# A decoder trunk on one core: which tick each segment of the next tile starts in, the tile's squares in tick 0, and the phase's sum ahead of the segment

## The chip, the core and the metric

The kernel runs on 1 core of one Trainium2 chip. The metric is the device time of one execution in microseconds (us), smaller is better. Engine names as in the profile: PE is TensorE's matmuls and PEld its weight loads, DVE is VectorE, ACT is ScalarE, POOL is GpSimd, SP is SyncE, which only issues DMAs here.

## What is computed

Two layers over 256 tokens of width 1024, everything in float32. Each layer is a mixing sub-layer (three kinds of heads over one projection) and a retrieval sub-layer (PEER): for each token 128 rows of a table of 16384 experts are fetched, weighed and added.

```python
for l in range(DEPTH):                                   # 2
    mod = silu(c) @ ada_w[l] + ada_b[l]
    h = rmsnorm(x, norm_mix_g[l]) * (1 + sc_m) + sh_m
    cols = h @ w_in[l]
    mix = concat([diff_attention(...), rwkv7_time_mix(...), forgetting_attention(...)]) @ w_out[l]
    x = x + g_m * mix
    h = rmsnorm(x, norm_ffn_g[l]) * (1 + sc_f) + sh_f
    x = x + g_f * peer_ffn(h, ...)
return rmsnorm(x, final_norm_g)

def peer_ffn(h, wq, subkeys, u_tab, v_tab):              # per token t
    eidx, gate = top 16 of the pair sums of two top 16s, for each of 8 heads
    act  = einsum('thkd,td->thk', u_tab[eidx], h)
    coef = gate * gelu(act)
    return einsum('thk,thkd->td', coef, v_tab[eidx])
```

## The kernel before

The 256 tokens are two tiles of 128, so two layers make four pairs of layer and tile, which the code calls phases (`PHASES` = 4, numbered 0 to 3). A phase fetches `SEL` = 128 expert rows for each token of its tile. One fetch brings 128 rows of 8 KB (u and v of one expert for each token, 1 MB) with an indirect DMA that GpSimd issues (L379) into a ring of `RING` = 9 slots. VectorE multiplies the u half with the hidden state and sums it (`row`, L1435), ScalarE applies the gelu (`activate`, L1042), VectorE makes the coefficient (`coefficients`, L1448), ScalarE spreads it over a diagonal (`diagonals`, L1050), and TensorE adds the v half, weighed by that diagonal, to a PSUM accumulator (`weigh`, L772). Only then is the slot free and GpSimd fetches the next row into it.

Two fetched rows make a tick, so a phase has `TICKS` = 64 of them. While phase p fetches and weighs, the same engines compute the mixing sub-layer and the retrieval's scores of the next phase's tile, cut into 79 segments (`SEGMENTS`, 0 to 78). The program of each engine is written out in Python: in tick m each engine does its part of the rows, then, through `beside.upto(PACE[m])`, its part of all segments up to number `PACE[m]`, then the rest of the tick. On VectorE the order in a tick is two rows, one part of the current tile's retrieval (ticks 0 to 23 alone, L1119 to L1157), the segments, the coefficients. On ScalarE it is the gelu, the segments, the diagonals. On TensorE it is the segments, then the weighing. Engines wait on one another by semaphores, in program order, so a wait in a segment holds everything behind it on its engine.

`pace()` makes the table from `COST`, a number for each segment. Before, segment n starts in tick `1 + 61 * done // 1783`, where `done` is the sum of the costs ahead of it. Phase 3 has no next tile; it only finishes tile 0. Phase 0's own mixing (of tile 0) runs ahead of all phases, about the first 290 us, and doesn't use this table.

The segments that the text speaks of:
- 0: ScalarE's sum of squares and square root (L809, L811), VectorE's copies. 1: VectorE's reciprocal (L1103), ScalarE's scaling (L816), TensorE's transposes (L394). 2: ScalarE and VectorE evict them (L821, L1171).
- 2 to 12, 15 to 20, 24 to 27: TensorE's projections, one group of eight matmuls each (L412); 13, 14 and 21 to 23 are the wide ones (L415). 26 is the first that needs the last group of weights, which SP loads once the projection of group `dv` (segment 23) is done (L322).
- 9: VectorE makes the squared keys (L1323) and TensorE sums them (L441). 10: VectorE takes the sums from PSUM (L1326).
- 16: VectorE's inputs for the forget gate and lambda; 17: ScalarE's exponentials and logarithm (L933 to L937).
- 28 to 30: TensorE's pair products (L482), which VectorE takes (L1192) in 29 to 31. 30 to 42: the attention and the levels of the block inverse, one unit a segment.
- 43 to 57: the state, the outputs, the output projection and the second norm. 57 to 74: the queries and scores. 75 to 77: the gate rows (L748, L795, L801).

At a phase's end, `add_sum` (L1456, L1457) reads the finished accumulator and adds it to x; it stands in tick 0 of the following phase, and TensorE's first weighing of that phase waits for it, since it reuses the accumulator.

## Time and profile before

| | us |
|---|---|
| median of 3 runs | 1900.18 |
| lowest and highest | 1897.82, 1906.14 |
| the profiled execution | 1903.03 |
| its span, first to last instruction | 1901.2 |
| PE busy | 1616.6 (85%) |
| DVE busy | 1394.7 (73%) |
| ACT busy | 673.4 (35%) |
| POOL busy | 515.2 (27%) |
| moved by DMA | 706.08 MB, mean 371 GB/s |

The profiled execution lies 2.85 us above the median. In it the first row of phase 0 is taken at 292 us; the coefficients of tick 0 of phases 0, 1, 2 and 3 end at 296.9, 725.5, 1146.7 and 1571.9 us. Busy shares are means over the whole span, and the stretches differ: the rows further down separate them.

### The profile page before, as it was taken

What the parts mean: (1) busy time and instruction counts of PE and PEld (TensorE: products, weight loads), DVE (VectorE), ACT (ScalarE), POOL (GpSimd) and SP (SyncE); (2) the same over time, 40 slices, a digit from 0 to 9 for tenths busy, and PEclk for the clock granted to TensorE, in tenths of its full rate; (3) what the DMA queues carried; (4) which work ended last, traced back from release to release, by engine and by line L of the source; (5) the groups of instructions that cost most, each with busy time, mean ns of one, the idle gap of its engine ahead of it and who ended that gap; (6) DMA issues with size and microseconds to landing.
All of it is one profiled execution on the core that took longest, in us unless ns stands there. A gap on an engine that the chain in (4) does not pass through costs nothing.

```text
span 1901.2 us, 20926 instructions
## 1 busy us (share of the span) xinstructions
PE 1616.6 (85%) x6868; PEld 1006.0 (53%) x6868; DVE 1394.7 (73%) x3315; ACT 673.4 (35%) x1640; POOL 515.2 (27%) x564
## 2 busy tenths in 40 slices
PE   1767678898999998898999998898999997887776
PEld 1656665554665655564665655554665652332222
DVE  5866598997856758998765748988765759985554
ACT  1313114334732334335632235325632233331112
POOL 2000013222233232222233232222232233343331
PEclk9889788998999999998999999999999998999999
DMA  9982688997799999998999999998899999999996
GB/s 393 422 346 101 242 353 348 367 421 286 283 399 421 422 420 395 363 422 313 321 403 421 421 421 399 370 402 293 287 403 421 421 415 401 416 407 421 421 421 256
DMA packets 96989, 706.08 MB, mean 371 GB/s; under 512 B 10992, under 2 KB 11504, under 8 KB 13296
## 3 DMA queue, kind: packets, MB, share of 16 engines
q0 software_dynamic: 80640, 587.24, 77.1%
q1 hardware_dynamic: 16240, 117.50, 15.1%
q8 instruction: 55, 0.90, 0.2%
q14 instruction: 54, 0.44, 0.1%
HBM read 703.64 MB, written 1.05 MB: 371 GB/s over the span
## 4 chain that ended last, share of the span: by engine, by line
PE 49%; DVE 28%; DMA 16%; ACT 3%; issue 3%; POOL 0%; DVEq 0%; ACTq 0%; POOLq 0%
PE psum L772 26%; DMA ringmem<-in_peer_uv_dram,eidx 11%; DVE ringmem L1435 9%; PE psum L648 5%; PE psum L412 4%; DMA W<-in_w_groups_dram 3%; PE psum L635 2%; DMA ringmem<-in_ada_pairs_dram 2%; PE psum L520 1%; PE psum L508 1%; DVE ringmem L1079 1%; PE psum L518 1%; PE psum L415 1%; DVE coef L1448 1%; ACT diag L1050 1%
## 5 line engine op out<-in xcount | busy, mean ns | idle before, releaser
L772 PE MATMUL psum<-ringmem,diag 128*128 128x512 f32 x2048 | 978.4, 624 | 132.3 <-ACT diag L1050 132.0
L379 POOL DMA_INDIRECT ringmem<-in_peer_uv_dram,eidx x512 | 489.5, 956 | 1131.5 <-PE psum L772 1079.7
L1435 DVE SCALAR_TENSOR_TENSOR ringmem<-ringmem,psum 128x1024 f32<-128x1024 f32 x512 | 612.5, 1220 | 195.3 <-DMA ringmem<-in_peer_uv_dram,eidx 180.1
L772 PEld LDWEIGHTS psum<-ringmem,diag 128*128 128x128 f32 x2048 | 389.1, 199 | 608.1 <-issue 409.1
L1050 ACT ACTIVATE diag<-K,coef 128x128 f32<-128x128 f32 x512 | 176.4, 393 | 225.8 <-DVE coef L1448 225.6
L412 PE MATMUL psum<-hT,W 128*128 128x128 f32 x1344 | 172.3, 287 | 40.9 <-DMA W<-in_w_groups_dram 19.1
L412 PEld LDWEIGHTS psum<-hT,W 128*128 128x128 f32 x1344 | 169.2, 203 | 64.9 <-issue 38.0
L1042 ACT ACTIVATE coef<-dots 128x2 f32<-128x2 f32 x256 | 51.8, 202 | 408.6 <-DVE ringmem L1435 407.7
L1079 DVE SCALAR_TENSOR_TENSOR ringmem<-ringmem,diag 128x1024 f32<-128x1024 f32 x96 | 115.3, 1223 | 20.9 <-DMA ringmem<-in_ada_pairs_dram 18.8
L648 PEld LDWEIGHTS psum<-hT,W 128*128 128x128 f32 x1024 | 123.2, 197 | 12.8 <-issue 7.2
L648 PE MATMUL psum<-hT,W 128*128 128x128 f32 x1024 | 126.0, 281 | 3.1 <-ACT hT L821 3.0
L1042 ACT ACT_TABLE_LOAD x80 | 102.6, 1283 | 1.4
L1448 DVE SCALAR_TENSOR_TENSOR coef<-coef,ginv,gexp 128x2 f32<-128x2 f32 x256 | 57.1, 223 | 47.5 <-ACT coef L1042 41.1
L370 POOL DMA_DIRECT2D ringmem<-in_ada_pairs_dram x48 | 25.5, 536 | 222.2 <-DVE ringmem L1079 221.4
L635 PE MATMUL psum<-W,hT 128*128 128x256 f32 x256 | 60.3, 393 | 0.8 <-issue 0.8
L635 PEld LDWEIGHTS psum<-W,hT 128*128 128x128 f32 x256 | 50.6, 198 | 13.7 <-issue 6.9
L1208 DVE COPY_PREDICATED W<-K,psum 128x384 f32<-128x384 int32 x32 | 18.7, 585 | 47.3 <-PE psum L553 47.3
L866 ACT ACTIVATE attn<-attn,ast 128x128 f32<-128x128 f32 (+1 forms) x64 | 28.7, 449 | 54.4 <-DVE ast L1223 53.7
L394 PE MATMUL psum<-K,hm 128*128 128x128 f32 x96 | 15.4, 313 | 38.2 <-ACT hm L816 27.9
L415 PE MATMUL psum<-W,hT 128*128 128x260 f32 (+1 forms) x128 | 41.0, 467 | 7.2 <-DMA W<-in_w_groups_dram 7.2
L1012 ACT ACTIVATE ar<-psum 128x256 f32<-128x256 f32 x32 | 12.2, 382 | 94.0 <-PE psum L648 94.0
L1192 DVE TENSOR_TENSOR W<-psum,K 128x512 f32<-128x512 f32 x24 | 16.6, 691 | 38.0 <-PE psum L482 37.5
(243 smaller groups left out, 1629.7 us busy)
## 6 DMA issues: line engine op xcount, KB each, us to landing
ringmem<-in_ada_pairs_dram POOLq DMA_DIRECT2D x48, 1024.0 KB, 19.0
W<-in_w_pieces_dram SPq DMA_DIRECT2D x48, 1024.0 KB, 9.2
W<-in_w_groups_dram SPq DMA_DIRECT2D x24, 1536.0 KB, 11.3
W<-in_w_groups_dram SPq DMA_DIRECT2D x12, 1024.0 KB, 9.6
ringmem<-in_peer_uv_dram,eidx POOLq DMA_INDIRECT x512, 11.7
W<-in_w_groups_dram SPq DMA_DIRECT2D x4, 1040.0 KB, 9.2
attn<-in_subkeys_t_dram SPq DMA_DIRECT2D x4, 1024.0 KB, 9.5
K<-in_consts_dram SPq DMA_DIRECT2D x1, 1546.0 KB, 18.1
```

What stands on the lines that cost most here:

```text
L379: nc.gpsimd.indirect_dma_start(slot(k), None, rows, bass.IndirectOffsetOnAxis(ap=eidx[:, ph % 2, m:m + 1], axis=0)).then_inc(row_landed[q ...
L412: mm = nc.tensor.matmul(group_bank(g)[:, j * P:(j + 1) * P], wt[:, k, j * P:(j + 1) * P], hT[:, k, :], start=(k == 0), stop=(k == KD - 1))
L415: mm = nc.tensor.matmul(group_bank(g)[:, 0:w], hT[:, k, :], wt[:, k, 0:w], start=(k == 0), stop=(k == KD - 1))
L635: mm = nc.tensor.matmul(bank[6 + j // 2][:, (j % 2) * 256:(j % 2 + 1) * 256], hT[:, k, :], wpiece[j % 3][:, k, :], start=(k == 0), stop=(k ...
L648: mm = nc.tensor.matmul(bank[6 + h % 2][:, a * P:(a + 1) * P], wpiece[j % 3][:, k, a * P:(a + 1) * P], hT[:, k, :], start=(k == 0), stop=( ...
L772: mm = nc.tensor.matmul(acc[:, q], diag[:, k % DIAGS, :], slot(k)[:, D:][:, q], start=(k % SEL == 0), stop=(k % SEL == SEL - 1), skip_grou ...
L866: ins = nc.scalar.activation(sc[:, n % 2, a, 0:nk], sc[:, n % 2, a, 0:nk], exp, bias=ast[:, n % 4, a:a + 1], scale=DIFF_SCALE if kind == " ...
L1042: nc.scalar.activation(coef[:, q], dots[:, q], gelu).then_inc(s["gelu_out"], 1)
L1050: ins = nc.scalar.activation(diag[:, k % DIAGS, :], ident, ACT.Copy, scale=coef[:, j:j + 1])
L1079: ins = v.scalar_tensor_tensor(out=u, in0=u, scalar=1.0, in1=crow, op0=ALU.mult, op1=ALU.mult, accum_out=MC[:, l, SECTIONS[r // KD], r % K ...
L1435: ins = v.scalar_tensor_tensor(out=u, in0=u, scalar=1.0, in1=hrep, op0=ALU.mult, op1=ALU.mult, accum_out=dots[:, j:j + 1])
L1448: step(v.scalar_tensor_tensor(out=coef[:, q], in0=coef[:, q], scalar=ginv[:, ph % 2, h:h + 1], in1=gexp[:, ph % 2, m * BATCH:(m + 1) * BAT ...
```

## The change

`pace()` now uses 62 instead of 61, has no 1 added, and lets each of the fourteen segments named in `CHAINED` start at least one tick after the segment ahead of it. On VectorE `add_sum` moves ahead of the segments of tick 0.

```diff
--- before.py
+++ after.py
@@ -96,11 +96,15 @@
 assert len(COST) == SEGMENTS
 
 
+
+CHAINED = {1, 2, 43, 44, 45, 46, 47, 48, 49, 50, 51, 55, 56, 57}
+
+
 def pace():
 
-    total, done, out = sum(COST), 0, [-1] * TICKS
+    total, done, tick, out = sum(COST), 0, 0, [0] * TICKS
     for n, w in enumerate(COST):
-        tick = 1 + (TICKS - 3) * done // total
+        tick = max((TICKS - 2) * done // total, tick + (n in CHAINED))
         for m in range(tick, TICKS):
             out[m] = n
         done += w
@@ -1487,9 +1491,9 @@
                             row(k)
                         if m < 4 * (PH - 2):
                             retrieve(ph, 2 + m // 4, m % 4)
-                        beside.upto(PACE[m])
                         if m == 0 and ph:
                             add_sum(ph - 1)
+                        beside.upto(PACE[m])
                         coefficients(n)
                 add_sum(PHASES - 1)
                 finish_tile(1)
```

What the table becomes (segments by tick):

| tick | 0 | 1 | 2 | 3 | 4 | 5 | 6 | 7 | 8 | 9 | 10 | 11 |
|---|---|---|---|---|---|---|---|---|---|---|---|---|
| before | | 0, 1, 2 | 3 | 4, 5 | 6 | 7 | 8, 9 | 10 | 11, 12 | 13 | 14 | 15, 16 |
| now | 0 | 1 | 2, 3, 4 | 5, 6 | 7 | 8 | 9, 10 | 11 | 12, 13 | 14 | 15 | 16, 17 |

| tick | 12 | 13 | 14 | 15 | 16 | 17 | 18 | 19 | 20 | 21 | 22 | 23 | 24 | 25 |
|---|---|---|---|---|---|---|---|---|---|---|---|---|---|---|
| before | 17 | 18 | 19 | 20, 21 | 22 | 23, 24 | 25, 26 | 27, 28 | 29 | 30 | 31 | 32 | 33 | 34 |
| now | 18 | 19 | 20, 21 | 22 | 23, 24 | 25, 26 | 27 | 28, 29 | 30 | 31 | 32 | 33 | 34 | |

Ticks 26 to 30 hold segments 35 to 39 in both. Before, tick 31 is empty and 40 to 45 stand in ticks 32 to 37, 46 and 47 together in tick 38. Now 40 to 46 stand in ticks 31 to 37 and 47 alone in 38. From there on the tables differ by at most one tick, and by the gate rows at the end: 75 in tick 60 and 76, 77 in tick 61 before, 75 and 76 in tick 60 and 77 in tick 61 now. Of the pairs that `CHAINED` takes apart, only 0, 1, 2 and 46, 47 shared a tick before.

**ScalarE where segment 0 of a next tile stands** (here the start of phase 1; L1042 is the gelu and L1050 the diagonals of a tick, L809 and L811 segment 0, L816 segment 1, L821 segment 2). Before:

```order
L1042 ACTIVATE coef<-dots 128x2
L1050 ACTIVATE diag<-K,coef 128x128 x2
L1042 ACTIVATE coef<-dots 128x2
L809 ACTIVATE hm,stat<-xs 128x1024
L811 ACT_TABLE_LOAD
L811 ACTIVATE stat<-stat 128x1
L816 ACTIVATE hm<-xs,stat 128x1024
L821 ACTIVATE hT<-psum,MC 128x128 x4
L1050 ACTIVATE diag<-K,coef 128x128 x2
L1042 ACT_TABLE_LOAD
```

Now (line numbers four higher: L1046, L1054, L813, L815, L820, L825):

```order
L1046 ACTIVATE coef<-dots 128x2
L813 ACTIVATE hm,stat<-xs 128x1024
L815 ACT_TABLE_LOAD
L815 ACTIVATE stat<-stat 128x1
L1054 ACTIVATE diag<-K,coef 128x128 x2
L1046 ACT_TABLE_LOAD
L1046 ACTIVATE coef<-dots 128x2
L820 ACTIVATE hm<-xs,stat 128x1024
L1054 ACTIVATE diag<-K,coef 128x128 x2
L1046 ACTIVATE coef<-dots 128x2
L825 ACTIVATE hT<-psum,MC 128x128 x4
```

The squares and the square root stand between the gelu and the diagonals of tick 0; the scaling and the eviction follow in ticks 1 and 2.

**TensorE over the same ticks and up to the sums of the keys** (L772 is the weighing, x4 is one tick; L394 the transposes, L412 the projections, L430 and L436 the low-rank inputs and the gate, L441 the key sums). Before:

```order
L412 MATMUL psum<-hT,W 128x128 x8
L772 MATMUL psum<-ringmem,diag 128x512 x4
L412 MATMUL psum<-hT,W 128x128 x16
L772 MATMUL psum<-ringmem,diag 128x512 x4
L412 MATMUL psum<-hT,W 128x128 x8
L430 MATMUL psum<-attn,lora 128x128 x3
L430 MATMUL psum<-mixed,lora 128x128 x3
L772 MATMUL psum<-ringmem,diag 128x512 x4
L412 MATMUL psum<-hT,W 128x128 x8
L436 MATMUL psum<-lora,attn 128x384
L772 MATMUL psum<-ringmem,diag 128x512 x4
L412 MATMUL psum<-hT,W 128x128 x16
L441 MATMUL psum<-T,K 128x384
```

Now (L776, L416, L434, L440, L445):

```order
L416 MATMUL psum<-hT,W 128x128 x16
L434 MATMUL psum<-attn,lora 128x128 x3
L434 MATMUL psum<-mixed,lora 128x128 x3
L776 MATMUL psum<-ringmem,diag 128x512 x4
L416 MATMUL psum<-hT,W 128x128 x8
L440 MATMUL psum<-lora,attn 128x384
L776 MATMUL psum<-ringmem,diag 128x512 x4
L416 MATMUL psum<-hT,W 128x128 x8
L776 MATMUL psum<-ringmem,diag 128x512 x4
L416 MATMUL psum<-hT,W 128x128 x8
L445 MATMUL psum<-T,K 128x384
L416 MATMUL psum<-hT,W 128x128 x8
```

The projections of one more segment stand ahead of each of the early weighings, a projection of the following segment stands behind the key sums in the same tick, and VectorE's reader of the sums is in this tick too, as the next rows show.

**VectorE around the sums of the keys** (L1323 writes the squares, L1326 reads the sums, L1448 ends a tick, L1435 begins the next). Before:

```order
L1182 SCALAR_TENSOR_TENSOR mixed<-mixed,pcols,colsT 128x128 x3
L1322 TENSOR_TENSOR T<-mixed,pcols 128x384
L1323 TENSOR_TENSOR T<-T 128x384
L1448 SCALAR_TENSOR_TENSOR coef<-coef,ginv,gexp 128x2
L1435 SCALAR_TENSOR_TENSOR ringmem,dots<-ringmem,psum 128x1024 x2
L1144 TENSOR_SCALAR fhi<-fpos 128x16
```

Now (L1327, L1330, L1452, L1439):

```order
L1186 SCALAR_TENSOR_TENSOR mixed<-mixed,pcols,colsT 128x128 x3
L1326 TENSOR_TENSOR T<-mixed,pcols 128x384
L1327 TENSOR_TENSOR T<-T 128x384
L1330 TENSOR_SCALAR T<-psum 128x384
L1333 SCALAR_TENSOR_TENSOR attn<-AL,pcols 128x384
L1334 SCALAR_TENSOR_TENSOR attn<-attn,mixed 128x384
L1452 SCALAR_TENSOR_TENSOR coef<-coef,ginv,gexp 128x2
L1439 SCALAR_TENSOR_TENSOR ringmem,dots<-ringmem,psum 128x1024 x2
```

The reader of the sums, which stood behind two rows and a retrieval part of the next tick, now stands directly behind the writer of the squares.

## Rows read from the trace of the kernel before

**Rows 1.** Stretches: the front (ticks 0 to 35) and back (36 to 63) of phases.
```profile
core 0: us, PE busy (x) PEld busy (x) DVE busy (x) ACT busy (x) POOL busy (x), PEclk, DMA share, GB/s
296.90:533.00 236.10, 217.89 (x948) 135.97 (x949) 198.22 (x501) 116.26 (x256) 63.72 (x66) 0.95 0.89 345
...
725.50:963.70 238.20, 220.51 (x968) 138.51 (x969) 202.10 (x520) 117.04 (x267) 65.76 (x69) 0.95 0.92 360
963.70:1146.70 183.00, 168.70 (x743) 106.36 (x741) 115.14 (x262) 55.20 (x147) 55.44 (x59) 0.99 1.01 420
1146.70:1389.70 243.00, 225.01 (x988) 141.01 (x989) 202.66 (x511) 118.51 (x263) 65.42 (x68) 0.95 0.90 350
```

**Rows 2.** The chain that ended last, phase 3, two fetches 16 ticks apart (start, length).
```profile
1758.26 15.10 DMA ringmem<-in_peer_uv_dram,eidx
...
1838.05 15.41 DMA ringmem<-in_peer_uv_dram,eidx
```

**Rows 3.** Timeline of ticks 0 and 1 of phase 1, engine by engine.
```profile
723.79 1.23 DVE L1457 TENSOR_TENSOR xs<-xs,hm 128x1024 f32<-128x1024 f32 x1
...
730.86 0.16 DVE L1103 RECIPROCAL stat<-stat 128x1 f32<-128x1 f32 x1 [0.59 <-ACT stat L811]
733.89 1.36 DVE L1171 TENSOR_SCALAR hT<-psum,MC 128x128 f32<-128x128 f32 x4 [2.87 <-PE psum L394]
...
728.02 1.04 ACT L809 ACTIVATE hm<-xs 128x1024 f32<-128x1024 f32 x1
...
729.17 1.28 ACT L811 ACT_TABLE_LOAD   x1
730.46 0.29 ACT L811 ACTIVATE stat<-stat 128x1 f32<-128x1 f32 x1
...
726.25 6.66 PE L772 MATMUL psum<-ringmem,diag 128*128 128x512 f32 x8 [5.08 <-ACT diag L1050]
...
735.36 2.02 PE L412 MATMUL psum<-hT,W 128*128 128x128 f32 x16 [1.58 <-ACT hT L821]
```

**Rows 4.** Timeline of PE, ticks 29 to 31: one weighing, then two back to back.
```profile
931.94 3.70 PE L772 MATMUL psum<-ringmem,diag 128*128 128x512 f32 x8
...
938.68 7.13 PE L772 MATMUL psum<-ringmem,diag 128*128 128x512 f32 x16
```

**Rows 5.** Timeline of PE and DVE around the sums of the keys, phase 1.
```profile
769.30 0.81 PE L441 MATMUL psum<-T,K 128*128 128x384 f32 x2
...
767.76 0.56 DVE L1323 TENSOR_TENSOR T<-T 128x384 f32<-128x384 f32 x1
...
774.38 0.56 DVE L1326 TENSOR_SCALAR T<-psum 128x384 f32<-128x384 f32 x1
```

**Rows 6.** Timeline of ACT, segment 17 in tick 12 of phase 1.
```profile
814.98 1.28 ACT L937 ACT_TABLE_LOAD   x1
```

**Rows 7.** Timeline of SP, PE and DVE around the last weight load, phase 1.
```profile
845.61 0.33 SPq L322 DMA_DIRECT2D W<-in_w_groups_dram  x1
...
854.74 3.48 PE L412 MATMUL psum<-hT,W 128*128 128x128 f32 x16 [2.16 <-DMA W<-in_w_groups_dram]
858.01 3.86 PE L772 MATMUL psum<-ringmem,diag 128*128 128x512 f32 x8
...
864.82 1.42 DVE L1192 TENSOR_TENSOR W<-psum,K 128x512 f32<-128x512 f32 x2 [6.55 <-PE psum L482]
```

**Rows 8.** Timeline of DVE, the ends of ticks 4 and 5 of phase 1.
```profile
753.10 0.22 DVE L1448 SCALAR_TENSOR_TENSOR coef<-coef,ginv,gexp 128x2 f32<-128x2 f32 x1
...
757.48 0.22 DVE L1448 SCALAR_TENSOR_TENSOR coef<-coef,ginv,gexp 128x2 f32<-128x2 f32 x1
```

**Rows 9.** The page's group of VectorE's row products: busy, mean ns.
```profile
L1435 DVE SCALAR_TENSOR_TENSOR ringmem<-ringmem,psum 128x1024 f32<-128x1024 f32 x512 | 612.5, 1220 | 195.3 <-DMA ringmem<-in_peer_uv_dram,eidx 180.1
```

**Rows 10.** Timeline of PE, the end of phase 3: the last gate row, the last three weighings.
```profile
1876.55 1.16 PE L748 MATMUL psum<-hm,ones 128*128 128x128 f32 x8 [0.85 <-ACT hm L795]
1878.97 12.26 PE L772 MATMUL psum<-ringmem,diag 128*128 128x512 f32 x24 [1.26 <-ACT diag L1050]
```

## The prediction

> **What bounds the kernel now.** I read the stretches by clock time first, since shares over the whole span mix unlike parts. A phase has a front, ticks 0 to 35, in which the transfers run at 345 to 360 GB/s, and a back, ticks 36 to 63, at 420 [rows 1]. In the front the ring is often full of landed rows that wait for VectorE and TensorE, so the DMA engines run dry; in the back VectorE waits for rows. The chain of waits shows what a tick costs when only transfers count: in phase 3 two fetches that stand 16 ticks apart begin at 1758.26 and 1838.05 us, so a tick is 4.99 us [rows 2]. Bytes are unchanged, so the time changes by what is added to or taken from the dry time of the fronts, and by the tail. One phase is worked out, phase 1; phases 0 and 2 have the same table and the same kinds of wait.
>
> **What a shift of the table is worth by itself.** The attention and the block inverse, which end the front, now stand one tick earlier: the last unit, segment 42, is in tick 33 instead of 34. So one tick without new work leaves the front and is done in the back. In the front it costs TensorE, which is busy there for 220.5 of 238.2 us [rows 1] and in the attention almost without a break, one weighing: two back to back take 7.13 where one takes 3.70, so 3.43 us [rows 4]. In the back it costs 4.99 us [rows 2]. This alone is 4.99 - 3.43 = +1.6 us a phase. It is the unobvious part: work done earlier in a tick count isn't done earlier in time if the tick it leaves was cheap.
>
> **The waits, as TensorE sees them at equal segments.**
>
> 1. Squares in tick 0. ScalarE now waits for the phase's sum (VectorE ends it at 723.79 + 1.23 = 725.02), then does squares, table load and root, which took 728.02 to 730.75, so 2.73 us, and only then the diagonals that release the first weighing. Before, the weighing began at 726.25, 1.23 behind the sum, with coefficients and diagonals in between. The coefficients (some 0.5 of it) can run beside the squares, the diagonals can't: 2.73 + 0.73 - 1.23, so 2.2, and I take 2.3 for a handover more; bounds 1.5 and 2.7. TensorE already waits 5.08 there [rows 3]. VectorE isn't held, its rows have landed.
> 2. What that removes: in tick 1 TensorE waited 1.58 for the evicted transposes and VectorE 0.59 + 2.87 = 3.46 for root and transposes [rows 3]. Both go. TensorE's net of items 1 and 2 is +0.7.
> 3. The key sums. VectorE wrote their input at 767.76 + 0.56 = 768.3 and read the sums at 774.38, behind the rows and a retrieval part of the next tick; TensorE made them from 769.30 to 770.1 [rows 5]. Now VectorE reads directly behind the write. It arrives 3.46 sooner, at 764.9 or, with smaller new waits for ScalarE's gelu and low-rank work in ticks 2 to 5, which I bound by 0 and 1.5, up to 766.4. TensorE has the same six weighings and projections ahead, so it is done at 770.1 + 0.7 = 770.8. VectorE thus waits about 5 us, more than it gained in tick 1; the gain of tick 1 is given back here. While it waits, the diagonals of tick 6 stand behind it. For TensorE the waits of ticks 6 to 10 stay about the same; I take -0.6, bounds -2 and +2.
> 4. Segments 16 and 17 share tick 11. ScalarE's exponential needs VectorE's result and TensorE's second transposes of the same tick, and then two table loads of 1.28 stand ahead of the diagonals [rows 6]. Before, segment 17 had a tick to itself, where the gate's exponential had loaded the first table. The order has three more table loads, one a phase. I take 2.3 us (1.28, the load, and 1.0 for the order within the tick), bounds 0 and 3.8 (the load, and one more load's length for each side of the handover).
> 5. The last weight load. SP issues it at 845.61 when group `dv` is done, TensorE starts on it at 854.74 after 2.16 of waiting [rows 7]. Segments 23 and 26 stay one tick apart, so this wait stays: 0.
> 6. Segments 30 to 33 now fall in ticks 20 to 23 and meet VectorE's last retrieval parts; before, 33 was in tick 24, free of them. VectorE picks up with the pair products (before at 864.82 [rows 7]) and then bounds these ticks. One more part must be done before segment 33: a tick with a part and no segment is 757.48 - 753.10 = 4.38 [rows 8], less two row products of 1.22 [rows 9] and the coefficients' 0.22, so 1.7. TensorE is also handed the pair products and the masks in one tick each; I take 2.2 in all, bounds 0 and 4.
>
> Sum a phase: 1.6 + 0.7 - 0.6 + 2.3 + 0 + 2.2 = +6.2 us, for three phases +18.6. Splitting 46 from 47 lies in the back, where transfers bound: 0. `add_sum` ahead of segment 0 puts VectorE's copies (under 0.5 us) behind the sum instead of into tick 1: 0; without the move ScalarE's squares would wait a little longer.
>
> **The tail.** Phase 3 has no segments but the gate rows. The second one ran at 1876.55, in tick 61, and the last three weighings ran back to back from 1878.97 to 1891.23, 12.26 us [rows 10]. With both gate rows in tick 60, the weighing of 61 can start sooner; the last rows set the end then: -1.7, bounds -2 and 0.
>
> **Sum.** 1903.03 + 18.6 - 1.7 = 1919.9 for the profiled execution, which is 2.85 above the median; so **1917 us**.
>
> **A rule weighed.** The table loads took 1.28 us, and the root began 0.01 after the load's end (729.17 + 1.28 = 730.45, then 730.46) [rows 3]. The Trainium skill (ScalarE: Activation LUTs, What ACT_TABLE_LOAD costs) gives 1283 ns and a drain of about 1380 ns, 2.66 us for a switch. The row shows no drain. By the page the three added loads would cost 4.1 us more, an estimate, and the sum would be about 1921.
>
> **Rivals.**
>
> A. *No net change* (1894 to 1908, likeliest 1901). New waits fall into VectorE's or TensorE's existing ones: the waits of items 4 and 6 are hidden by TensorE's backlog, and the shift's +1.6 is all that stays: 3 x 1.6 - 1.7 = +3. For it: TensorE trails VectorE by some microseconds through ticks 11 to 20, and backlog hides releases. Against it: in tick 20 the trail ends, VectorE waits 6.55 for TensorE [rows 7].
>
> B. *Faster, through tick 1* (about 1888). The wait of 3.46 on VectorE [rows 3] is really gone and isn't given back, because TensorE reaches the key sums sooner than item 3 has it. Then VectorE is 3.5 ahead, SP issues the last load that much earlier, and the wait of 2.16 [rows 7] goes too: 1.6 - 3.5 - 2.2 = -4.1 a phase, -12.3 and the tail. It decides if VectorE's wait for the key sums stays under 1.5 us. For it: TensorE's 1.58 goes. The Trainium skill (Perfetto Trace Analysis, Optimization Strategies) speaks for it: where TensorE idles for other engines, shorten what blocks it. Here the trace agrees only in that tick; the hold of item 1 lengthens another of TensorE's idle times.
>
> C. *The change hardly does what it says* (within 3 us of 1900). Of fourteen names only two groups shared a tick before. The shift of the others is real, though, as the order shows, so this is weak.
>
> **How the numbers follow.** My forecast 0.50 (1909 to 1930: bounds of items 3, 4 and 6 together), A 0.26, B 0.20, C 0.04. A measurement of this kernel can tell 0.5%, 9.5 us, from no change. Faster by over 0.5%: B and a little of A, 0.20. Slower by over 0.5%: the forecast with a little left off at its low end and a little of A added, 0.51. Within: 0.29. The range leaves out half of B below 1888 and the forecast's end above 1930: 1888 to 1930; the forecast's own is 1909 to 1930.
>
> **What would show it.** Right: VectorE has waits of 4 to 6 us for L445 in tick 6 of each phase; no wait at L1175 in tick 1 of more than 0.5; TensorE's first weighing of phases 1 and 2 begins about 2.3 later against the end of the sum; the coefficients of tick 35 come 5 to 8 us later after those of tick 0; the backs keep 420 GB/s. Wrong: fronts shorter than 236 to 243 us [rows 1] at equal ticks, a wait for L445 under 1.5, or dry transfers in the back. A back with waits on TensorE while rows lie landed would make the whole split by front and back wrong.

## The result and the profile after

| | us |
|---|---|
| before, median of 4 runs | 1899.0 (1897.1 to 1906.1) |
| the changed kernel, median of 4 runs | 1921.3 (1920.9 to 1922.8) |
| ratio, 95% interval | 1.0102, 1.0082 to 1.0122 |
| profiled execution and its span, before | 1903.0, 1901.2 |
| profiled execution and its span, after | 1920.9, 1919.1 |

The changed kernel is slower by 1.0%, some 19 us. The forecast was 1917. Where the 17.9 us between the two spans lie can be read from the ends of the coefficients (L1448 before, L1452 after) of tick 0 and tick 35 of each phase:

| | before | after | longer by |
|---|---|---|---|
| start to tick 0 of phase 0 | 296.9 | 300.0 | 3.1 |
| phase 0, to tick 0 of phase 1 | 428.6 | 432.3 | 3.7 |
| of it ticks 0 to 35 | 244.2 | 246.9 | 2.7 |
| phase 1, to tick 0 of phase 2 | 421.2 | 427.3 | 6.0 |
| of it ticks 0 to 35 | 236.0 | 241.6 | 5.6 |
| phase 2, to tick 0 of phase 3 | 425.2 | 428.9 | 3.7 |
| of it ticks 0 to 35 | 244.2 | 247.6 | 3.4 |
| phase 3, to the last coefficients | 313.1 | 315.0 | 1.9 |
| from there to the end | 16.2 | 15.7 | -0.5 |

So 13.4 us were lost in the three phases that have segments, 11.7 of them in the fronts. The 3.1 ahead of phase 0 and the 1.9 in phase 3 lie where both kernels run the same instructions, apart from the squares in tick 0 and the gate rows; the last section comes back to them. The fronts of this table end with the coefficients of tick 35; the windows of [rows 1] end elsewhere, that of phase 0 at 533.0 where tick 35 ends at 541.1, so its 236.10 is not comparable with the 244.2 here.

Stretches of the changed kernel's phase 1, front and back, as in [rows 1]; the columns are PE, PEld, DVE, ACT and POOL busy, then the granted clock, the DMA share and GB/s:

```profile
732.30:974.10 241.80, 219.76 (x968) 137.76 (x969) 199.81 (x517) 118.23 (x267) 64.61 (x68) 0.94 0.90 350
974.10:1159.50 185.40, 168.72 (x742) 105.99 (x740) 116.97 (x264) 54.83 (x149) 56.52 (x60) 1.00 1.01 421
```

The back still runs at 421 GB/s, and the front is longer with the same work: TensorE is busy for 219.8 us of 241.8, against 220.5 of 238.2 [rows 1]. The loss is waiting.

Timeline of the start of phase 1 after the change (start, length, engine, line; in brackets the idle time before it and what ended it):

```profile
729.93 1.23 DVE L1461 TENSOR_TENSOR xs<-xs,hm 128x1024 f32<-128x1024 f32 x1
...
742.58 1.37 DVE L1175 TENSOR_SCALAR hT<-psum,MC 128x128 f32<-128x128 f32 x4
...
731.18 1.06 ACT L813 ACTIVATE hm<-xs 128x1024 f32<-128x1024 f32 x1 [4.04 <-DVE xs L1461]
...
732.35 1.28 ACT L815 ACT_TABLE_LOAD   x1
733.65 0.29 ACT L815 ACTIVATE stat<-stat 128x1 f32<-128x1 f32 x1
733.85 0.68 ACT L1054 ACTIVATE diag<-K,coef 128x128 f32<-128x128 f32 x2
...
734.58 5.92 PE L776 MATMUL psum<-ringmem,diag 128*128 128x512 f32 x8 [6.83 <-ACT diag L1054]
```

The phase's sum ends at 731.16 and the first weighing begins at 734.58, 3.42 behind it; before it was 726.25 - 725.02 = 1.23 [rows 3]. So item 1 costs 2.2, as forecast. And L1175, which waited 2.87 in tick 1 before [rows 3], now takes the transposes in tick 2 and waits for nothing.

Timeline of ticks 6 and 7 of phase 1 after the change, VectorE and then TensorE:

```profile
770.92 0.56 DVE L1327 TENSOR_TENSOR T<-T 128x384 f32<-128x384 f32 x1
775.62 0.56 DVE L1330 TENSOR_SCALAR T<-psum 128x384 f32<-128x384 f32 x1 [4.15 <-PE psum L445]
...
785.58 2.55 DVE L1338 RECIPROCAL T<-T 128x384 f32<-128x384 f32 x1
...
789.35 0.22 DVE L1452 SCALAR_TENSOR_TENSOR coef<-coef,ginv,gexp 128x2 f32<-128x2 f32 x1
...
774.70 0.81 PE L445 MATMUL psum<-T,K 128*128 128x384 f32 x2
775.35 1.95 PE L416 MATMUL psum<-hT,W 128*128 128x128 f32 x16
778.40 3.70 PE L776 MATMUL psum<-ringmem,diag 128*128 128x512 f32 x8 [1.10 <-ACT diag L1054]
781.94 1.95 PE L416 MATMUL psum<-hT,W 128*128 128x128 f32 x16
790.35 5.35 PE L776 MATMUL psum<-ringmem,diag 128*128 128x512 f32 x8 [6.46 <-ACT diag L1054]
```

VectorE stands 4.15 us for the keys' sums, and one tick later TensorE stands 6.46 for the diagonals, which wait for VectorE's coefficients at 789.57. That wait is an old one: TensorE of the kernel before, ticks 7 to 9 of phase 1:

```profile
777.16 3.70 PE L772 MATMUL psum<-ringmem,diag 128*128 128x512 f32 x8 [1.83 <-ACT diag L1050]
780.70 3.73 PE L412 MATMUL psum<-hT,W 128*128 128x128 f32 x32
789.84 5.59 PE L772 MATMUL psum<-ringmem,diag 128*128 128x512 f32 x8 [5.41 <-ACT diag L1050]
795.26 1.92 PE L415 MATMUL psum<-W,hT 128*128 128x260 f32 x8
```

In tick 8 TensorE waits 5.41 for VectorE. The prediction never looked at this row, and it is the one that decided two of its items.

TensorE of the changed kernel in ticks 21 to 23 of phase 1, where the attention meets VectorE's last retrieval parts:

```profile
885.01 0.71 PE L537 MATMUL psum<-dk,dq 64*128 64x128 f32 x4 [1.86 <-DVE ast L1227]
886.51 6.75 PE L776 MATMUL psum<-ringmem,diag 128*128 128x512 f32 x8 [0.79 <-ACT diag L1054]
...
901.21 0.94 PE L512 MATMUL psum<-W 128*128 128x128 f32 x6 [2.08 <-DVE W L1204]
...
903.16 1.22 PE L537 MATMUL psum<-dk,dq 64*128 64x128 f32 x4 [0.62 <-DVE ast L1227]
904.65 6.22 PE L776 MATMUL psum<-ringmem,diag 128*128 128x512 f32 x8 [0.28 <-ACT diag L1054]
```

VectorE bounds these ticks, and two weighings that took 3.70 elsewhere [rows 4] took 6.75 and 6.22 behind the waits. The kernel before has two slow ones there as well, of 5.36 and 5.40.

### The profile page after: what moved, and what is told of

It reads as the page before. It is cut to its first block, busy times and chain, and to the rows that moved or that the text cites. A ratio compares the mean times of both kernels' runs of the same rounds, so it can differ in the third digit from the quotient of the medians.

```text
span 1919.1 us, 20926 instructions
## 1 busy us (share of the span) xinstructions
PE 1619.7 (84%) x6868; PEld 1009.7 (53%) x6868; DVE 1394.0 (73%) x3315; ACT 678.6 (35%) x1643; POOL 517.6 (27%) x564
## 4 chain that ended last, share of the span: by engine, by line
PE 53%; DVE 23%; DMA 17%; ACT 3%; issue 3%; POOL 0%; DVEq 0%; ACTq 0%; POOLq 0%
PE psum L776 29%; DMA ringmem<-in_peer_uv_dram,eidx 12%; DVE ringmem L1439 7%; PE psum L416 5%; PE psum L652 4%; DMA W<-in_w_groups_dram 3%; PE psum L639 2%; DMA ringmem<-in_ada_pairs_dram 2%; PE psum L419 2%; PE psum L524 1%; DVE ringmem L1083 1%; PE psum L512 1%; PE psum L522 1%; PE psum L752 1%; DVE W L1196 1%
## 5 line engine op out<-in xcount | busy, mean ns | idle before, releaser
L776 PE MATMUL psum<-ringmem,diag 128*128 128x512 f32 x2048 | 976.3, 623 | 140.3 <-ACT diag L1054 140.0
L1439 DVE SCALAR_TENSOR_TENSOR ringmem<-ringmem,psum 128x1024 f32<-128x1024 f32 x512 | 613.2, 1220 | 236.4 <-DMA ringmem<-in_peer_uv_dram,eidx 219.9
L776 PEld LDWEIGHTS psum<-ringmem,diag 128*128 128x128 f32 x2048 | 388.6, 198 | 614.0 <-issue 407.2
L1054 ACT ACTIVATE diag<-K,coef 128x128 f32<-128x128 f32 x512 | 176.4, 393 | 201.9 <-DVE coef L1452 197.9
L1046 ACT ACTIVATE coef<-dots 128x2 f32<-128x2 f32 x256 | 51.9, 203 | 469.0 <-DVE ringmem L1439 462.3
L416 PE MATMUL psum<-hT,W 128*128 128x128 f32 x1344 | 168.0, 282 | 34.5 <-DVE hT L1175 17.2
L416 PEld LDWEIGHTS psum<-hT,W 128*128 128x128 f32 x1344 | 165.2, 198 | 59.6 <-issue 37.7
L1452 DVE SCALAR_TENSOR_TENSOR coef<-coef,ginv,gexp 128x2 f32<-128x2 f32 x256 | 57.0, 222 | 49.9 <-ACT coef L1046 43.8
L1439 DVE DVE_READ_ACCUMULATOR ringmem<-ringmem,psum 128x1 f32 x512 | 42.3, 83 | 0.0
L512 PE MATMUL psum<-W 128*128 128x128 f32 x240 | 36.3, 291 | 7.1 <-DVE W L1204 7.1
```

The costliest lines, as they stand in the source:

```text
L416: mm = nc.tensor.matmul(group_bank(g)[:, j * P:(j + 1) * P], wt[:, k, j * P:(j + 1) * P], hT[:, k, :], start=(k == 0), stop=(k == KD - 1))
L512: mm = nc.tensor.matmul(bank[5][:, j * P:(j + 1) * P], AT[b][:, 0:P], X[:, b, :], start=True, stop=True)
L776: mm = nc.tensor.matmul(acc[:, q], diag[:, k % DIAGS, :], slot(k)[:, D:][:, q], start=(k % SEL == 0), stop=(k % SEL == SEL - 1), skip_grou ...
L1046: nc.scalar.activation(coef[:, q], dots[:, q], gelu).then_inc(s["gelu_out"], 1)
L1054: ins = nc.scalar.activation(diag[:, k % DIAGS, :], ident, ACT.Copy, scale=coef[:, j:j + 1])
L1439: ins = v.scalar_tensor_tensor(out=u, in0=u, scalar=1.0, in1=hrep, op0=ALU.mult, op1=ALU.mult, accum_out=dots[:, j:j + 1])
```

## The experiments

`pace()` can be written as a plain list of each segment's tick. In the experiments it is (`BEGINS`, with `return [sum(s <= m for s in BEGINS) - 1 for m in range(TICKS)]`), and each diff shows the lines of that list that differ: a line that begins with 0 holds segments 0 to 25, one that begins with 17 or 18 segments 26 to 51. All runs stood beside runs of the kernel before on the same chip; the ratio is to those.

| run | base | edit | median us | ratio, 95% interval |
|---|---|---|---|---|
| `e_chain` | before | 0, 1, 2 in ticks 0, 1, 2; sum ahead | 1890.8 | 0.9951, 0.9932 to 0.9969 |
| `e_keys` | changed | 10 in tick 7 | 1910.4 | 1.0049, 1.0032 to 1.0066 |
| `e_gate` | changed | 17 in tick 12 | 1923.3 | 1.0120, 1.0102 to 1.0138 |
| `e_attn` | changed | 29 to 34 and 40 to 46 a tick later | 1899.2 | 0.9991, 0.9979 to 1.0003 |
| `b_pairs` | before | 29 to 34 a tick earlier | 1915.4 | 1.0083, 1.0062 to 1.0104 |
| `b_outputs` | before | 40 to 46 a tick earlier | 1907.1 | 1.0034, 1.0021 to 1.0048 |
| `a_sum` | changed | sum behind the segments | 1923.1 | 1.0119, 1.0100 to 1.0139 |
| `e_both` | changed | `e_keys` and `e_attn` | 1886.3 | 0.9933, 0.9912 to 0.9954 |
| `e_root` | `e_both` | 2 in tick 1 | 1896.7 | 0.9976, 0.9966 to 0.9986 |
| `e_early` | `e_both` | 40 to 46 a tick earlier | 1891.0 | 0.9939, 0.9921 to 0.9957 |
| `e_late` | `e_chain` | 29 to 39 a tick later | 1888.4 | 0.9937, 0.9916 to 0.9958 |
| `e_free` | `e_both` | 29 to 39 a tick later | 1876.6 | 0.9863, 0.9844 to 0.9883 |

In what follows a difference of two ratios is given in us of 1900; each is uncertain by 4 to 5.

### The split of the chain alone

```diff
-        1, 1, 1, 2, 3, 3, 4, 5, 6, 6, 7, 8, 8, 9, 10, 11, 11, 12, 13, 14, 15, 15, 16, 17, 17, 18,
+        0, 1, 2, 2, 3, 3, 4, 5, 6, 6, 7, 8, 8, 9, 10, 11, 11, 12, 13, 14, 15, 15, 16, 17, 17, 18,
...
-                        beside.upto(PACE[m])
                         if m == 0 and ph:
                             add_sum(ph - 1)
+                        beside.upto(PACE[m])
```

> The kernel before with the sum ahead of the segments and segments 0, 1 and 2 in ticks 0, 1 and 2; all the others where they were. Theory T (the loss comes from the segments that were moved a tick earlier, and the split of the chain is a small cost on TensorE in tick 0 against a wait gone in tick 1): 1897 to 1903 us, within 0.3% of the kernel before; VectorE and TensorE have no wait over 0.5 us for the squares in tick 1, and the keys' sums are read one tick after they are written with no long wait. Rival B (VectorE's 3.5 us of waiting in tick 1 was worth its length in each phase): 1888 or less. Rival H (the squares in front of the first weighing are what costs): 1907 or more.

Measured 1890.8, 9 us faster than before. My theory and its value fell, and the value of B was near, but not by B's whole path: the wait for the last weights, which B took away, is still 2.01 in phase 1 of this run. The wait of tick 8 after this edit, TensorE, phase 1:

```profile
784.62 5.73 PE L771 MATMUL psum<-ringmem,diag 128*128 128x512 f32 x8 [5.05 <-ACT diag L1049]
```

Against the end of the coefficients of tick 0 (724.29, before 725.47) this weighing begins at 60.33, before at 64.37: 4.0 earlier. The gain stood at 1.6 from tick 3 to 6, became 4.0 in tick 8 and stayed that to the end of the phase. In phase 0 it is 1.5 and then 3.6. In phase 2 the weighings of ticks 3 to 6 come 0.5 later, and from tick 8 on 3.1 earlier. So VectorE's gain in tick 1 reaches TensorE in full, at the place where TensorE waits for VectorE.

### Which of the two waits in tick 1 it was

`e_root` puts segment 2 back beside 1; it is cut from `e_both` (below), which holds the split of the chain and no wait for the keys.

```diff
-        0, 1, 2, 2, 2, 3, 3, 4, 5, 6, 7, 7, 8, 8, 9, 10, 11, 11, 12, 13, 14, 14, 15, 16, 16, 17,
+        0, 1, 1, 2, 2, 3, 3, 4, 5, 6, 7, 7, 8, 8, 9, 10, 11, 11, 12, 13, 14, 14, 15, 16, 16, 17,
```

> e_both with segments 1 and 2 together in tick 1 (0 stays in tick 0). It parts the two waits of VectorE in tick 1 of the kernel before: 0.59 for the root stays away, 2.87 for the transposes comes back. Theory V (VectorE bounds tick 8, so what it gains in tick 1 arrives there in full): 2 to 3.5 us a phase more than e_both, 1893 to 1897. Rival (TensorE's idle time for the first weighing decides, and VectorE's waits in tick 1 are covered): 1885 to 1889.

Measured 1896.7, by ratio 8 us slower than `e_both`. VectorE in tick 1 of phase 1:

```profile
730.58 1.36 DVE L1174 TENSOR_SCALAR hT<-psum,MC 128x128 f32<-128x128 f32 x4 [5.24 <-PE psum L397]
```

With the squares in tick 0 TensorE is later, so the wait for its transposes is 5.24 where it was 2.87. Against `e_both` the coefficients of ticks 6 to 20 come 5.3 to 5.6 later and the first weighing that shows the whole of it is that of tick 7; 3.5 are left at the end of the phase; the three phases are 4.9, 3.5 and 5.1 longer. VectorE's time ahead of tick 7 is worth its length there, and it is the transposes' wait that the split pays by; the root's 0.59 is away in `e_root` too.

### The sum's place

```diff
-                        if m == 0 and ph:
-                            add_sum(ph - 1)
                         beside.upto(PACE[m])
+                        if m == 0 and ph:
+                            add_sum(ph - 1)
```

> The changed kernel with the sum behind the segments again, where the kernel before had it; nothing else. By the forecast (VectorE's copies of under 0.5 us stand ahead of the sum, and ScalarE's squares, if they follow the sum, wait that much longer): +0.5 us a phase over three phases, 1921 to 1924 us. If ScalarE's squares no longer wait for the sum: up to 3 us less a phase, 1912 or more. If the copies hold nothing: 1921.

Measured 1923.1, by ratio 3 us slower than the changed kernel, which its interval does not part from none. In phase 1 the weighings of ticks 1 to 9 come 0.7 to 0.8 later. That is all that can be put down to the move: over whole phases the run is 4.6 longer in phase 0, which has no sum to move, 1.0 shorter in phase 1 and 1.9 longer in phase 2.

### The keys' sums

```diff
-        0, 1, 2, 2, 2, 3, 3, 4, 5, 6, 6, 7, 8, 8, 9, 10, 11, 11, 12, 13, 14, 14, 15, 16, 16, 17,
+        0, 1, 2, 2, 2, 3, 3, 4, 5, 6, 7, 7, 8, 8, 9, 10, 11, 11, 12, 13, 14, 14, 15, 16, 16, 17,
```

> The changed kernel with segment 10 in tick 7 instead of 6, so that VectorE reads the keys' sums one tick after it writes the squares. Theory T as forecast (item 3: the wait of 4 to 5 us on VectorE is hidden by TensorE's backlog): 1919 to 1923 us, no change. Rival K (that wait holds the diagonals of tick 6 and the rows behind it, and TensorE loses with it): 2 to 4 us less a phase, 1909 to 1915.

Measured 1910.4, by ratio 10 us faster than the changed kernel. My item 3 fell, K holds. VectorE takes the sums without a wait, and TensorE's next wait is shorter:

```profile
771.58 0.56 DVE L1329 TENSOR_SCALAR T<-psum 128x384 f32<-128x384 f32 x1
...
780.17 3.70 PE L775 MATMUL psum<-ringmem,diag 128*128 128x512 f32 x8 [3.47 <-ACT diag L1053]
```

3.47 where it was 6.46. In phase 1 the weighings of ticks 8 to 10 come 3.8 to 4.1 earlier than in the changed kernel: the 4.15 of L1330. Not all of it stays: from tick 12 on it is 2.1, and the three phases are 1.8, 1.8 and 3.6 shorter, 7.2 in all where the ratio says 10.

### The gate's two segments in one tick

```diff
-        0, 1, 2, 2, 2, 3, 3, 4, 5, 6, 6, 7, 8, 8, 9, 10, 11, 11, 12, 13, 14, 14, 15, 16, 16, 17,
+        0, 1, 2, 2, 2, 3, 3, 4, 5, 6, 6, 7, 8, 8, 9, 10, 11, 12, 12, 13, 14, 14, 15, 16, 16, 17,
```

> The changed kernel with segment 17 in tick 12 instead of 11, so that the forget gate's inputs and its exponentials have a tick of their own each. As forecast in item 4, worth 2.3 us a phase: 1914 us, between 1910 and 1921. If the tick's wait is made up later (the weighings stood 3.4 later in tick 11 but coefficients only 0.6 to 1.9 in ticks 11 and 12): 1920 to 1922.

Measured 1923.3: nothing gained, if anything 3 lost. The wait of item 4 is there in the changed kernel, as ScalarE and TensorE of tick 11 show:

```profile
817.58 1.28 ACT L937 ACT_TABLE_LOAD   x1
...
819.19 1.28 ACT L941 ACT_TABLE_LOAD   x1
...
821.33 3.70 PE L776 MATMUL psum<-ringmem,diag 128*128 128x512 f32 x8 [2.17 <-ACT diag L1054]
```

TensorE stands 2.17 in tick 11, and with the edit that weighing comes 2.4 earlier after the coefficients of tick 0. But the weighing of tick 12 comes where it came: segment 17's own work now stands there and takes what was won. Item 4's 2.3 us a phase was the price of one tick, not of the phase. The run also has six table loads fewer than the changed kernel, 174 against 180, and is no faster.

### The later segments: pairs and attention

```diff
-        17, 18, 19, 19, 20, 21, 22, 23, 24, 26, 27, 28, 29, 30, 31, 32, 33, 34, 35, 36, 37, 38, 39, 40, 41, 42,
+        17, 18, 19, 20, 21, 22, 23, 24, 25, 26, 27, 28, 29, 30, 32, 33, 34, 35, 36, 37, 38, 38, 39, 40, 41, 42,
```

> The changed kernel with segments 29 to 46 one tick later, where the kernel before had them. By items 6 and the shift of the forecast this gives back 2.2 + 1.6 us a phase, in all 11 us: 1910 us (1904 to 1916). If the loss is made ahead of tick 19 and only shows there: 1918 to 1922.

Measured 1899.2: all of the loss is gone, 21 us, twice what items 6 and the shift were held to be worth. Two kernels cut it from the other side. `b_pairs`, from the kernel before:

```diff
-        18, 19, 19, 20, 21, 22, 23, 24, 25, 26, 27, 28, 29, 30, 32, 33, 34, 35, 36, 37, 38, 38, 39, 40, 41, 42,
+        18, 19, 19, 19, 20, 21, 22, 23, 24, 26, 27, 28, 29, 30, 32, 33, 34, 35, 36, 37, 38, 38, 39, 40, 41, 42,
```

> The kernel before with segments 29 to 34 alone one tick earlier (29 now shares tick 19 with 27 and 28, and the free tick moves from 31 ahead to 25; both stay). By item 6 of the forecast 2.2 us a phase, in all +7: 1907 us. By e_attn's trace, whose loss of 5 us a phase against the changed kernel stands between ticks 19 and 26: +10 to +15, 1910 to 1915. If the pieces only cost together with segments 9 to 28 being early: under +4.

Measured 1915.4, 16 us slower than before; the forecast's 2.2 a phase is half of what it costs, or less. Its trace says why. VectorE in tick 19 and TensorE in ticks 21 and 22, phase 1:

```profile
869.92 1.42 DVE L1191 TENSOR_TENSOR W<-psum,K 128x512 f32<-128x512 f32 x2 [11.21 <-PE psum L481]
...
884.17 0.71 PE L532 MATMUL psum<-dk,dq 64*128 64x128 f32 x4 [1.87 <-DVE ast L1222]
...
891.24 0.52 PE L494 MATMUL psum<-K,W 128*128 128x128 f32 x3 [1.87 <-DVE W L1199]
```

Segment 29 takes the pair products that TensorE makes in the same tick. VectorE, a tick ahead, has to stand 11.21 for them, and in tick 20 the wait of 6.55 [rows 7] is not taken again. What is worse, the following ticks are VectorE's (two rows, a retrieval part and a unit of the attention; ticks 21 to 23 take 7.0 to 9.5 us each), and it enters them later. In phase 1 the weighings of ticks 22 and 23 come 6.6 to 6.9 later than before, and 3.7 of it stays.

The changed kernel itself doesn't show 11.21. There the projections are a tick earlier too, and its wait has to be held against that of `e_attn`, the same kernel with the pairs back where the kernel before has them. The changed kernel and then `e_attn`, VectorE, phase 1:

```profile
870.77 1.42 DVE L1196 TENSOR_TENSOR W<-psum,K 128x512 f32<-128x512 f32 x2 [6.53 <-PE psum L486]
```

```profile
866.14 1.42 DVE L1195 TENSOR_TENSOR W<-psum,K 128x512 f32<-128x512 f32 x2 [2.13 <-PE psum L485]
```

So in phase 1 the shared tick adds 4.4 to this wait here and 4.7 between `b_pairs` and the kernel before; in phases 0 and 2 it is 2.5 to 4.3. At tick 30 the loss is 5.2, 3.7 and 4.1 in phases 0 to 2 by `b_pairs` and 2.6, 5.1 and 5.6 by `e_attn`, 13 in all both times, beside the 16 of the ratio. No run moves segment 29 alone, so how much of it is this wait and how much the units that meet VectorE's last retrieval parts stays open.

`b_outputs`, the shift with no other effect:

```diff
-        18, 19, 19, 20, 21, 22, 23, 24, 25, 26, 27, 28, 29, 30, 32, 33, 34, 35, 36, 37, 38, 38, 39, 40, 41, 42,
+        18, 19, 19, 20, 21, 22, 23, 24, 25, 26, 27, 28, 29, 30, 31, 32, 33, 34, 35, 36, 37, 38, 39, 40, 41, 42,
```

> The kernel before with segments 40 to 46 alone one tick earlier, so tick 31 is no longer free of segments. By the forecast's first term (a cheap tick leaves the front, 1.6 us a phase): +5, 1905 us. If a shift inside the front that adds no wait costs nothing: 1899 to 1902.

Measured 1907.1, 6.5 us slower, near the forecast's 4.8. But its profiled execution doesn't show where: phases 0 to 2 are 0.6 and 0.6 longer and 0.6 shorter than before. So it was measured a second time on another base, `e_both`, with the same edit:

```diff
-        17, 18, 19, 20, 21, 22, 23, 24, 25, 26, 27, 28, 29, 30, 32, 33, 34, 35, 36, 37, 38, 38, 39, 40, 41, 42,
+        17, 18, 19, 20, 21, 22, 23, 24, 25, 26, 27, 28, 29, 30, 31, 32, 33, 34, 35, 36, 37, 38, 39, 40, 41, 42,
```

> e_both with segments 40 to 46 one tick earlier, the second measure of the shift alone. If b_outputs' 6.7 us are the shift's own: 1892 to 1894. If they are not, as its trace says (its phases 0 to 2 are 0.6, 0.6 and -0.6 us longer than those of the kernel before): 1885 to 1889.

Measured 1891.0, between the two; by ratio 1.1 us slower than `e_both`. From tick 31 on, where the edit begins, its phases 0, 1 and 2 are 1.8, 0.3 and 0.1 longer. A third reading is `e_attn`, which gives back 1.4, 1.3 and 3.8 behind tick 30. The shift alone is a loss of 1 to 6 us in all. That it is one is likely, and its size stays open.

### Both repairs, and what is left of the change

```diff
-        0, 1, 2, 2, 2, 3, 3, 4, 5, 6, 6, 7, 8, 8, 9, 10, 11, 11, 12, 13, 14, 14, 15, 16, 16, 17,
-        17, 18, 19, 19, 20, 21, 22, 23, 24, 26, 27, 28, 29, 30, 31, 32, 33, 34, 35, 36, 37, 38, 39, 40, 41, 42,
+        0, 1, 2, 2, 2, 3, 3, 4, 5, 6, 7, 7, 8, 8, 9, 10, 11, 11, 12, 13, 14, 14, 15, 16, 16, 17,
+        17, 18, 19, 20, 21, 22, 23, 24, 25, 26, 27, 28, 29, 30, 32, 33, 34, 35, 36, 37, 38, 38, 39, 40, 41, 42,
```

> The changed kernel with both edits that gained: segment 10 in tick 7 and segments 29 to 46 one tick later. Against the kernel before it still has the split of the chain and segments 3 to 9 and 11 to 28 up to one tick earlier. Theory T (three separate terms: chain -10, sums of the keys +11, segments 29 to 46 +22; the rest of the shift costs nothing): 1888 to 1893 us, as e_chain. Theory U (the earlier segments 11 to 28 also cost, and only overlap with the other two): 1894 or more. If the two edits give back the same wait: 1899.

Measured 1886.3, 13 us faster than before and 3 to 4 faster than `e_chain`. The terms are separate and add up. What `e_both` has beyond `e_chain` costs nothing that shows and may gain a little: most of segments 3 to 8 and 11 to 28 stand a tick earlier, so that 16 and 17 share one, and so do five segments of the back and one gate row. Its front of phase 1 beside [rows 1]:

```profile
718.70:950.00 231.30, 215.71 (x962) 135.59 (x963) 199.04 (x515) 118.07 (x266) 64.84 (x68) 0.96 0.93 369
```

### One tick more between the pairs and the attention

`e_late` puts segments 29 to 39 a tick later in `e_chain`, so that the tick without a segment is 20 and not 31:

```diff
-        18, 19, 19, 20, 21, 22, 23, 24, 25, 26, 27, 28, 29, 30, 32, 33, 34, 35, 36, 37, 38, 38, 39, 40, 41, 42,
+        18, 19, 19, 21, 22, 23, 24, 25, 26, 27, 28, 29, 30, 31, 32, 33, 34, 35, 36, 37, 38, 38, 39, 40, 41, 42,
```

> e_chain with segments 29 to 39 one tick later, so that the free tick stands at 20 instead of 31. Theory T (VectorE's last retrieval parts and its wait for the pair products make ticks 20 to 23 the dearest; each tick that the pairs move away from them gives back): 3 to 5 us a phase less than e_chain, 1877 to 1882. Rival (in e_chain the trail is already free at tick 20, so an empty tick there is worth what one at 31 is): 1889 to 1893. Rival (VectorE's wait of 6.5 us in tick 20 stays, for the pair products of segment 28 are late for TensorE's own reasons): 1886 to 1890.

Measured 1888.4, 2 to 3 us faster than `e_chain`, which is not parted from none. VectorE in tick 20 of its phase 1:

```profile
859.83 0.22 DVE L1447 SCALAR_TENSOR_TENSOR coef<-coef,ginv,gexp 128x2 f32<-128x2 f32 x1 [7.86 <-ACT coef L1041]
```

ScalarE ahead of it:

```profile
857.20 0.38 ACT L846 ACTIVATE fk<-psum 128x256 f32<-128x256 f32 x1 [9.90 <-PE psum L411]
```

The wait for the pairs only changed its name: VectorE now stands 7.86 for ScalarE's gelu, which stands behind ScalarE's eviction of TensorE's last projection. In `e_both` the projections are a tick earlier, and there the same edit is `e_free`:

```diff
-        17, 18, 19, 20, 21, 22, 23, 24, 25, 26, 27, 28, 29, 30, 32, 33, 34, 35, 36, 37, 38, 38, 39, 40, 41, 42,
+        17, 18, 19, 21, 22, 23, 24, 25, 26, 27, 28, 29, 30, 31, 32, 33, 34, 35, 36, 37, 38, 38, 39, 40, 41, 42,
```

> e_both with segments 29 to 39 one tick later, so that the tick free of segments is 20 and not 31. Theory W (TensorE's waits of 1.9, 0.8 and 0.8 us in ticks 22 and 23 of e_both come from VectorE's last retrieval parts there, and the attention's first units leave them): 1 to 2 us less a phase, 1880 to 1884. Rival (as in e_late, the waits move with the units and only change their place): 1885 to 1888.

Measured 1876.6 over 4 runs, 13 us by ratio faster than `e_both` and 26 faster than the kernel before; more than W held. Its profiled execution, of 1883.6, is the longest of the four, so the trace shows less of it: phase 0 is 1.3 longer and phases 1 and 2 are 2.8 and 1.7 shorter than those of `e_both`. VectorE's wait for the pairs, 2.0 to 2.2 a phase in `e_both`, is gone. Where the rest of the 13 lies was not seen. TensorE in ticks 22 to 24 of phase 1:

```profile
871.14 3.70 PE L775 MATMUL psum<-ringmem,diag 128*128 128x512 f32 x8
874.68 0.49 PE L498 MATMUL psum<-K,W 128*128 128x128 f32 x3
877.73 0.71 PE L536 MATMUL psum<-dk,dq 64*128 64x128 f32 x4 [2.56 <-DVE ast L1226]
879.23 5.40 PE L775 MATMUL psum<-ringmem,diag 128*128 128x512 f32 x8 [0.79 <-ACT diag L1053]
884.46 0.49 PE L498 MATMUL psum<-K,W 128*128 128x128 f32 x3
```

One such wait, and one slow weighing, are left where the kernel before and the changed kernel each had two slow weighings. This is the version that beats both.

## Why the time was right and half of the sum was not

The sign, the size (1917 against 1921) and the place, the fronts of phases 0 to 2, came as forecast. The sum behind it did not: its terms were wrong in both directions and met in the total, and that they met is luck. In us over the three phases:

| term | forecast | measured by |
|---|---|---|
| items 1 and 2, split of the chain | +2.1 | -9 (`e_chain`) |
| item 3, keys' sums | -1.8 | +10 (`e_keys`) |
| item 4, gate | +6.9 | 0, or -3 (`e_gate`) |
| item 6, pairs and attention | +6.6 | +16 (`b_pairs`) |
| shift of 40 to 46 alone | +4.8 | +1 to +6 (`e_early`, `b_outputs`) |
| rest of the shift, with item 4 and the tail in it | 0 | -3 (`e_both` less `e_chain`) |
| tail | -1.7 | none seen |

The right column, with item 4 counted once, adds up to between 15 and 20, against 19 by the ratio; each entry is uncertain by 4 to 5.

Of the signs that the prediction named, VectorE's wait for L445 is there in each phase (4.0, 4.2 and 4.7), the wait at L1175 is gone, the first weighings of phases 1 and 2 stand 2.2 later against the sum, and the backs keep 419 to 421 GB/s. One sign failed: tick 35 was to come 5 to 8 us later in each phase and came 2.7, 5.6 and 3.4 later. Phase 1, the one worked out, was the dearest. So the phases carry 13.4 of the 18.6 that they were given, and a good part of the rest of the 17.9 between the two spans lies where nearly the same instructions run.

**Items 1 and 2.** The hold itself was right: 2.2 us measured in the trace. The step that failed is "TensorE's net of items 1 and 2 is +0.7": by `e_chain` the weighings of ticks 3 to 6 come 1.5 and 1.6 earlier in phases 0 and 1, and only phase 2 has 0.5 later. It priced the chain on TensorE in ticks 0 and 1 and dropped VectorE's 3.46 as if it had slack. But TensorE waits for VectorE in ticks 7 and 8 (1.83 and 5.41), so VectorE's time ahead of tick 8 counts in full. `e_chain` and `e_root` show it, in opposite directions.

**Item 3.** The wait was forecast well (about 5, measured 4.15), and so was its cause. The step that failed is "For TensorE the waits of ticks 6 to 10 stay about the same". It compared VectorE's arrival with TensorE's in tick 6 alone. The sentence before it, that the gain of tick 1 is given back here, was right, and together items 1 to 3 came near: forecast +0.3, measured about +1. So two errors were one: a gain and a loss on VectorE, both taken for nothing.

**Item 4.** The mechanism is in the trace (two loads of 1.28, a wait of 2.17), but the tick after hides it. It should have been asked which wait ends last in the next tick.

**Item 5** held. The same wait for the last weights is in the changed kernel, one tick earlier, TensorE and the granted clock of the stretch behind it:

```profile
858.90 2.05 PE L416 MATMUL psum<-hT,W 128*128 128x128 f32 x16 [2.11 <-DMA W<-in_w_groups_dram]
...
858.90:861.00 2.10, 2.10 (x17) 2.08 (x18) 2.07 (x6) 0.39 (x3) 0.00 (x0) 1.00 1.04 433
```

2.11 of waiting, before 2.16 [rows 7].

**Item 6** had the right place and half the size or less: 2.2 a phase, measured 4.3 to 5.3. The step that failed is the count of VectorE's work in ticks 20 to 23 as the whole price. It left out that segment 29 now shares a tick with the products that it reads, which adds 4.4 to VectorE's wait in phase 1 (6.53 against 2.13 in `e_attn`) before those ticks begin.

**The shift** of 1.6 a phase is in keeping with both measurements and shown by neither.

**The tail.** Both gate rows now stand in tick 60, but TensorE reaches its last weighings no sooner. Ends of the two kernels, the sum's first instruction before and after:

```profile
1891.33 1.23 DVE L1456 TENSOR_TENSOR hm<-psum,grow 128x1024 f32<-128x1024 f32 x1 [6.32 <-PE psum L772]
```

```profile
1892.59 1.91 PE L752 MATMUL psum<-hm,ones 128*128 128x128 f32 x8 [1.85 <-ACT hm L799]
1894.29 14.85 PE L776 MATMUL psum<-ringmem,diag 128*128 128x512 f32 x32
...
1909.24 1.22 DVE L1460 TENSOR_TENSOR hm<-psum,grow 128x1024 f32<-128x1024 f32 x1 [5.77 <-PE psum L776]
```

The second gate row's matmuls run back to back with four weighings instead of three [rows 10]. From the last coefficients to the end it is 0.5 us shorter, but `b_pairs` and `e_chain`, which have the gate rows of the kernel before, are 1.7 and 1.1 shorter there. From tick 0 of phase 3 to the end the five kernels with the old rows take 328.9 to 332.0 and the nine with the new ones 329.4 to 332.1. So no gain shows, and none of 1.7 came.

**The rivals.** A asked for hidden waits, and item 4's was hidden, but not those on VectorE. B named its condition, VectorE's wait for the keys under 1.5 us. The wait was 4.15, so B did not come. But the condition doesn't decide it alone: in `e_keys`, which makes just that true, the kernel runs at 1910, since B had no term for the pairs. Only with the pairs back in their tick as well, in `e_both`, is it 1886, near B's 1888. And the wait for the last weights, for which B took 2.2 a phase away, is in all fourteen kernels, 2.0 to 3.7 in each phase, so B's number was met by another sum.

**The sums themselves.** B's terms with the tail give 1903.0 - 12.3 - 1.7 - 2.85 = 1886, not 1888, and A's +3 gives 1903, not 1901. The bounds of items 3, 4 and 6 together span 1899 to 1935, not 1909 to 1930; the result lies in both.

**The rule of the Trainium skill on table loads** (ScalarE: Activation LUTs, What ACT_TABLE_LOAD costs) would add a drain of about 1.4 us to each load. The trace after disagrees as that of before did: L815's load ends at 732.35 + 1.28 = 733.63 and the root begins at 733.65. Over all loads of either trace ScalarE's median idle time is 0.02 ahead of a load and 0.01 behind it. That the sum with the drain, about 1921, is what was measured is chance, since no drain shows in either trace. The other rule of the Trainium skill, to shorten what blocks an idle TensorE (Perfetto Trace Analysis, Optimization Strategies), agrees with `e_chain`, though the wait that the edit shortened on VectorE was paid out seven ticks later.

## What to carry to other kernels

When engines run one in-order schedule, price a change of one engine's time at the next place where the bounding engine waits for it, not in the tick where it happens: look down the trace for the first long wait with that engine's name. A table that moves many segments by one tick is many edits; run its pieces alone, since here a gain of 9 and losses of 10 and 16 lay in one change of 19. And leave a tick between a product and its reader where the reader's engine runs ahead: the keys' sums show it alone, the pairs together with the units behind them.

## What was not expected of the hardware

**The clock behind a wait is not the wait's alone.** Stretches of 2 to 7 us in which TensorE ran right behind a wait, first the last weights of the kernel before, then two of the changed kernel (the granted clock is the third number from the end, of which 1.00 is 2.4 GHz):

```profile
854.70:858.30 3.60, 3.56 (x17) 3.56 (x18) 3.38 (x12) 0.00 (x0) 0.00 (x0) 0.56 1.03 428
```

```profile
790.40:795.80 5.40, 5.40 (x11) 2.48 (x12) 5.12 (x16) 1.79 (x4) 0.94 (x1) 0.69 0.00 0
...
886.50:893.30 6.80, 6.79 (x10) 2.90 (x11) 6.35 (x19) 2.74 (x3) 0.95 (x1) 0.54 0.55 187
```

After a wait of 2.16 sixteen matmuls took 3.48 at 0.56, nearer to the lower level of 1.2 GHz than to the upper; after one of 2.11, in the changed kernel, they took 2.05 at 1.00. A weighing took 5.35 behind a wait of 6.46 and 6.75 behind waits of 1.86 and 0.79. The two waits for weights are of nearly one length, and behind one of them the matmuls took 1.43 more and behind the other nothing; the weighing behind 2.65 of waits took 3.05 more than 3.70. What decides it these runs don't show. The sums above had no term for it.

**Stretches with the same instructions differ by some us.** The part ahead of phase 0, the same in all kernels, ended between 295.4 and 300.9 us in the twelve profiled executions of the experiments, at 296.9 before and 300.0 after. Of the stretch from 150 to 200 us, before and after:

```profile
150.00:200.00 50.00, 39.06 (x283) 35.91 (x284) 31.77 (x72) 17.36 (x54) 2.11 (x4) 0.93 0.31 107
```

```profile
150.00:200.00 50.00, 39.16 (x256) 35.96 (x256) 30.15 (x69) 16.62 (x52) 1.58 (x3) 0.86 0.31 106
```

The clock is 0.93 in one and 0.86 in the other. And phase 0 of `a_sum`, whose instructions are the changed kernel's, took 436.9 us against 432.3. One profiled execution does not price an edit of under 5 us in all. The ratios, uncertain by 4 to 5 between two runs, hardly do either; a row that differs alike in three phases is the better evidence.
